# Feed-forward weights: stationary columns taken with a step of two, down rows loaded in the matching order

## What is computed

```python
def swiglu(h, w_gate_up, w_down):
    g, u = jnp.split(h @ w_gate_up, 2, axis=-1)
    return (jax.nn.silu(g) * u) @ w_down
```

## Time and profile before

| | us |
|---|---|
| time, median of 3 runs (2536.79 to 2537.70) | 2537.19 |
| the profiled execution, its own time | 2537.48 |
| its span, first to last instruction | 2535.7 |
| TensorE busy in it | 2472.9 |
| VectorE busy | 1790.7 |
| ScalarE busy | 1396.0 |
| GpSimd busy | 243.3 |

### The profile page before, as it was taken

How to read it: one execution, slowest core, us unless ns; L and a number is a source line. 1 busy time by engine, 2 the same in 40 slices (tenths; PEclk the granted TensorE clock), 3 DMA queues, 4 the chain that set the end, 5 groups by cost and what they waited for, 6 DMA issues and landing times.

```text
span 2535.7 us, 41986 instructions
## 1 busy us (share of the span) xinstructions
PE 2472.9 (98%) x16447; PEld 2290.4 (90%) x16447; DVE 1790.7 (71%) x2196; ACT 1396.0 (55%) x1971; POOL 243.3 (10%) x383
## 2 busy tenths in 40 slices
PE   7899999999999999999999899999999999999998
PEld 6789999899999998999999799999999999999997
DVE  6769975675666797667667776666676676688765
ACT  3654447644555666556545565555565565576653
POOL 4221011200100122000000100000010000022000
PEclk8999999999999999999999999999999999999999
DMA  9549954375566455665565366566556556544553
GB/s 379 195 144 378 367 195 143 117 268 196 193 211 204 160 165 179 205 204 195 199 204 169 117 208 203 183 214 202 204 188 212 199 192 204 193 158 153 196 199 133
DMA packets 349342, 509.09 MB, mean 201 GB/s; under 512 B 9413, under 2 KB 302364, under 8 KB 345116
## 3 DMA queue, kind: packets, MB, share of 16 engines
q1 hardware_dynamic: 344080, 494.89, 57.5%
q0 software_dynamic: 4320, 11.47, 1.2%
q10 hardware_dynamic: 812, 0.91, 0.1%
HBM read 505.40 MB, written 1.84 MB: 200 GB/s over the span
## 4 chain that ended last, share of the span: by engine, by line
PE 85%; DVE 6%; ACT 4%; issue 2%; DMA 2%; POOL 0%; DVEq 0%; SPq 0%; ACTq 0%
PE B L664 20%; PE B L665 10%; PE Y L625 9%; PE Y L626 9%; PE Y L627 9%; PE B L625 7%; PE B L627 7%; PE B L626 7%; DVE w_lo L2108 2%; ACT w_hi L1500 2%; DVE M L2118 1%; DMA M<-in_w_ada 1%; ACT h_both L1596 1%; ACT junk L1525 1%; PE B L1000 1%
## 5 line engine op out<-in xcount | busy, mean ns | idle before, releaser
L2108 DVE TENSOR_TENSOR w_lo<-raw,w_hi 128x2048 fp32r<-128x2048 f32 (+1 forms) x412 | 939.1, 2280 | 187.7 <-ACT w_hi L1500 187.4
L1500 ACT ACTIVATE w_hi<-raw 128x2048 fp32r<-128x2048 f32 (+1 forms) x413 | 781.3, 1895 | 361.6 <-PE B L665 211.4
L664 PE MATMUL B<-h_both,w_hi 128*128 128x512 f32 x2304 | 760.5, 382 | 0.0
L665 PE MATMUL B<-h_both,w_lo 128*128 128x256 f32 x2304 | 628.0, 273 | 0.0
L664 PEld LDWEIGHTS B<-h_both,w_hi 128*128 128x128 f32 x2304 | 435.5, 189 | 60.3
L665 PEld LDWEIGHTS B<-h_both,w_lo 128*128 128x128 f32 x2304 | 442.2, 192 | 1.7
L625 PE MATMUL B<-h_both,w_hi 128*128 128x256 f32 x1356 | 376.3, 278 | 8.5 <-DVE w_lo L2108 7.6
L627 PE MATMUL B<-h_both,w_lo 128*128 128x256 f32 x1356 | 372.9, 275 | 0.0
L626 PE MATMUL B<-h_both,w_hi 128*128 128x256 f32 x1356 | 372.9, 275 | 0.0
L2118 DVE TENSOR_TENSOR xn<-B,xn 128x256 f32<-128x256 f32 (+1 forms) x296 | 114.2, 426 | 295.2 <-ACT xn L1519 289.9
L625 PE MATMUL Y<-w_hi,a_hi 128*128 128x512 f32 x812 | 308.3, 380 | 0.0
(11 more groups left out here) (372 smaller groups left out, 3514.3 us busy)
## 6 DMA issues: line engine op xcount, KB each, us to landing
raw<-in_ffn_w_in SPq DMA_DIRECT2D x176, 1024.0 KB, 5.0
raw<-in_ffn_w_out SPq DMA_DIRECT2D x88, 1024.0 KB, 4.9
raw<-in_w_gate_up SPq DMA_DIRECT2D x44, 1024.0 KB, 6.4
M<-in_w_ada SPq DMA_DIRECT2D x37, 1024.0 KB, 9.0
raw<-in_hgrn_w_in SPq DMA_DIRECT2D x32, 1024.0 KB, 5.2
raw<-in_w_down SPq DMA_DIRECT2D x22, 1024.0 KB, 5.0
raw<-in_w_in SPq DMA_DIRECT2D x14, 1024.0 KB, 6.4
raw<-in_diff_w_in SPq DMA_DIRECT2D x12, 1024.0 KB, 5.1
```

What stands on the lines that cost most here:

```text
L664: pe.matmul(B[banks[c]], hi[:, s], h_both[:, k].rearrange("p t a j -> p (a j) t"), start=k == 0, stop=False)
L665: mm = pe.matmul(B[banks[c]][:, 0:S], lo[:, s], tokens_of(h_hi[:, k]), start=False, stop=k == KD - 1)
L1500: act.activation(w_hi[st.n % RING][:, 0:n], raw[st.r % RING][:, 0:n], ACT.Copy).then_inc(unit_rounded, 1)
L2108: dve.tensor_tensor(w_lo[s][:, 0:n], raw[st.r % RING][:, 0:n], w_hi[s][:, 0:n].bitcast(F32), ALU.subtract).then_inc(unit_split, st.step("" ...
```

## The change

The stationary columns of gate and up are taken with a step of two: half c of a chunk is columns c, c + 2, c + 4 and so on, 128 of 256, in all chunks but the first. Down units from the second on are loaded so that partition p, block k gets row 2p + k, which is the row that belongs to column 2p + k. The first chunk's down unit keeps its order, and so do the mixers' calls of `stationary`.

```diff
                 def down(i):
-                    load(wdn[bass.ds(i * CH, CH), :].rearrange("(k p) n -> p k n", p=P), 2)
+                    load(wdn[bass.ds(i * CH, CH), :].rearrange("(p k) n -> p k n", p=P), 2)
...
-                down(0)
+                load(wdn[0:CH, :].rearrange("(k p) n -> p k n", p=P), 2)
...
-            def stationary(o, name, ready=None, kt=KD, halfway=None):
+            def together(k, c):
+                return slice(k * CH + c * P, k * CH + c * P + P)
+
+            def apart(k, c):
+                return slice(k * CH + c, k * CH + CH, 2)
+
+            def stationary(o, name, ready=None, kt=KD, halfway=None, columns=together):
...
-                        s = slice(k * CH + c * P, k * CH + c * P + P)
+                        s = columns(k, c)
                         mm = mm3(o[:, c * S:c * S + S], hi[:, s], lo[:, s], tokens_of(h_hi[:, k]), tokens_of(h_lo[:, k]),
                                  k == 0, k == kt - 1)
...
                     for k in range(KD):
-                        s = slice(k * CH + c * P, k * CH + c * P + P)
+                        s = apart(k, c)
                         pe.matmul(B[banks[c]], hi[:, s], h_both[:, k].rearrange("p t a j -> p (a j) t"), start=k == 0, stop=False)
...
-                        stationary(B[0], f"{p}.{tag}.gate")
+                        stationary(B[0], f"{p}.{tag}.gate", columns=apart)
                         pe.wait_ge(vector_step, st.at(f"{p}.{prev}.{'up_joined' if folded(p) else 'mul'}", back))
-                        stationary(B[1], f"{p}.{tag}.up")
+                        stationary(B[1], f"{p}.{tag}.up", columns=apart)
...
-                    stationary(B[0], f"{p}.second.gate")
+                    stationary(B[0], f"{p}.second.gate", columns=apart)
...
-                    stationary(B[1], f"{p}.second.up")
+                    stationary(B[1], f"{p}.second.up", columns=apart)
```

## The result

| | before | after |
|---|---|---|
| time, median of 4 runs each on one chip, us | 2536.99 | 2566.43 |
| ratio to before, 95% interval | | 1.0116 (1.0104 to 1.0129) |
| span of the profiled execution, us | 2535.7 | 2565.4 |
| TensorE busy, us | 2472.9 | 2502.9 |

The change makes the kernel 29.4 us (1.2%) slower, well beyond the interval. That is not the forecast (no change, 2537.2); it is the first rival, the slower stepped load, and lies within the range of 2525 to 2580.

What follows compares the result with a forecast made beforehand. TensorE's issue rhythm was taken to bound the kernel. Profiled 2537.48 us plus 4992 x 0 for loads and 0 for DMAs gave 2537.5, put at 2537.2 after the runs' median; range 2525 to 2580 us.

Steps and rivals of the forecast that it cites:

- What bounds the kernel: TensorE's issue rhythm sets the time, busy 2472.9 of 2535.7 us; moving columns bound, with the weight load right behind.
- The count of exposed and hidden loads: Gate and up weight loads: 4992 beside 256-column products exposed, 2304 beside 512-column ones hidden; 4.99 us per ns.
- (b) The down loads: DRAM order of the down rows: -0.1 to +0.1 us a load, between -0.8 and +0.7 us in all, taken as 0.
- (a) x = 0: Stepped weight loads of gate and up: x, the extra ns per load, taken as 0 for all 4992 exposed loads.
- rival 1: Stepped loads in wide and plain units somewhat slower: 9 ns each gives 2582 us, 4 ns gives 2557; chance 0.33.
- The upper bound: Most a stepped load could lengthen, from contiguous moving reads: 9 ns, or 4 ns by the per-column price.
- The page weighed: Documentation rule for SBUF reads: two successive accesses in one 16-byte line give full performance, so 0 ns; not taken as settling it.
- Rival 2: Stepped load removes the 2 to 3 ns turnaround between loads: 13.0 us gained, 2524 us; chance 0.14.
- Rival 3: Stepped load reads one word per access, doubling its 107 ns: 534 us more, 3071 us; chance 0.06.
- The signs to look for: Changed profile: loads still 189 and 192 ns, wide pair 328, plain products 111 to 112, down units 216 ns.

## Why the prediction went as it did

**What bounds the kernel** was right. Every nanosecond in TensorE's rhythm counted in full, and no other engine took part: 6 ns on each load without cover make 29.6 us, where 29.4 were measured.

**The count of exposed and hidden loads** was right but for the 64 wide loads behind a down unit (4928 exposed, not 4992; 0.4 us). 2304 hidden loads cost nothing when stepped (ratio 0.9996), and the exposed ones cost +14.6 us (wide) and +15.8 us (plain).

**(b) The down loads** at 0: right as far as the runs can tell, ratio 0.9997 alone (0.9987 to 1.0006).

**(a) x = 0** is the step that failed: the pace of a load does depend on its addresses, and x measured 6 ns. The range held the time because it was drawn to take in rival 1, not because this step was right. The argument was that a pace of one column in 0.83 ns that holds under every product looks set by the array and not by the memory. The rows showed that pace only under products of 64 columns; beside 256 and 512 the moving columns take as long or longer, and hide it. And an even pace of the contiguous load says only that its addresses don't slow it. By the price of a piece, 32 x 1.84 = 59 ns would do for it, an estimate (no run shows so short a load), 48 ns under the 107. So the even pace told nothing of how near the limit is. The step of two needs 118 ns for its pieces against 107 to 111 ns, and falls just over it.

**The upper bound** (4 to 9 ns from contiguous moving reads) held the 6 ns, and rested on the right likeness: a stepped load and a contiguous moving read of 256 columns pass the same addresses in the same time. Both touch 64 pieces, or 65 at 260 columns, 120 ns, which is 1.85 ns a piece. With hindsight the rows held the number: 120/65 = 1.85, and the load by that price 64 x 1.85 = 118 ns, +7 against 111. The prediction priced it per column (4 ns) and as a difference (9 ns), and did not take the price as a floor beside the array's; so it put this rival at 0.33, below the 0.47 of no change.

**The page weighed** (the Trainium skill, "Advanced Engine Details and Errata", SBUF Cachelines) is borne out better than the prediction allowed. One word in each 16-byte line doubled the load (236 ns), two in each did little harm; but its "full performance" at two is off by 6 to 7 ns here, and this is what the change costs. Nor do four in each give it on the moving side, where 512 contiguous columns took 229 ns in place of 216.

**Rival 2** (a gain of 2.7 ns) fell: no distance became shorter (117 to 118 ns in the plain units, 224 + 109 in the pair). **Rival 3** (a load twice as long) fell for the step of two, but steps of four and more cost about as much (221 to 239 ns a load).

**The signs to look for.** The prediction had rival 1 show in the distance after the 256-column product. It showed after the 512-column one, since a product is recorded as started while its own load is still under way. The down units kept their rhythm, as said; the timeline of the kernel after has six distances in 1.29 us, 215 ns each:

```profile
709.68 0.38 PE L625 MATMUL Y<-w_hi,a_hi 128*128 128x512 f32 x1
...
710.97 0.38 PE L670 MATMUL B<-h_both,w_hi 128*128 128x512 f32 x1
```

## What to carry to other kernels

Where two limits act at once (here the load's own 107 ns and the price of its pieces), only the larger one shows: an even pace tells which limit holds now, not what a new access pattern will meet. Before a stationary operand of 4-byte words is read with a step, count the 16-byte pieces it touches and the time of the product beside which its load runs: here 1.84 ns a piece against 109 ns beside 256 moving columns and 216 beside 512, so that the same step cost 6 ns in one place and nothing in the other. In this kernel the new order of rows was free in the DMA (ratio 0.9997) and not in the load of the stationary operand (1.0116).

## What was not expected of the hardware

- A load of 128 stationary columns of fp32r takes about 1.84 ns for each 16-byte piece of a partition, where that is more than the 107 to 111 ns of a contiguous load: 118, 177 and 236 ns for 64, 96 and 128 pieces. A contiguous read of moving columns shows a like price (120 ns for 260, 229 ns for 512), and one from two places in turn doesn't (216 ns for 512). At 128 pieces it varied from 221 to 239 ns with the step, for no reason that was found.
- A product's start is recorded before its weights are all loaded (0.12 us into a load of 0.236 us at step four). The delay then stands in the distance to the next product, at the product whose load was late (218 to 224 ns at 512 columns), not at the one before it (109 ns up to a step of three; 130 at step four, where the load of w_lo is late as well).
